# A hybrid decoder step on one core: the output projection taken by weight chunk, V caches loaded by chunk, and six smaller moves of loads and work

## The reference

```python
z = rmsnorm(x, g_mix) @ w_in                 # 1024 -> 3592 columns
attn_out = attn_fn(heads(aq), ak, av)        # 8 heads, mixture of windows (128,1) (512,4) (2048,16)
h_m, C, n, m = mlstm_chunked(...)            # 4 heads, matrix memory
h_h, S_new = hgrn2_chunked(...)              # 4 heads, gated linear recurrence
mlstm_out = sigmoid(mo) * head_rmsnorm(h_m, mlstm_g)
hgrn_out = sigmoid(hg) * head_rmsnorm(h_h, hgrn_g)
x = x + concat([attn_out, mlstm_out, hgrn_out]) @ w_out      # 1024 x 1024
u = rmsnorm(x, g_ffn) @ w_up                                 # 1024 -> 4096
x = x + square(relu(u)) @ w_down                             # 4096 -> 1024
```

## Time and profile before

| | |
|---|---|
| time, median of 3 runs | 1718.2 us (1717.47 to 1721.23) |
| the profiled execution's own time | 1717.58 us |
| its span | 1715.7 us |
| mean granted clock of TensorE | 0.967 of full |
| busy: PE, DVE, ACT, POOL | 91%, 50%, 28%, 14% of the span |

### The profile page before, as it was taken

How to read it: one execution, slowest core, us unless ns; L and a number is a source line. 1 busy time by engine, 2 the same in 40 slices (tenths; PEclk the granted TensorE clock), 3 DMA queues, 4 the chain that set the end, 5 groups by cost and what they waited for, 6 DMA issues and landing times.

```text
span 1715.7 us, 25329 instructions
## 1 busy us (share of the span) xinstructions
PE 1566.2 (91%) x10513; PEld 1372.4 (80%) x10513; DVE 857.8 (50%) x1493; ACT 480.1 (28%) x942; POOL 238.8 (14%) x341
## 2 busy tenths in 40 slices
PE   4899999799999798877499899999999999999997
PEld 3899889698889566663378788888889888888886
DVE  4682544066664277642734444444444444444446
ACT  4342221222211267631421322122122222212213
POOL 4421111687621000000500000000000000000000
PEclk9899999899999899989699999999999999999999
DMA  5322002712111832068300211111111111111102
GB/s 159 126 71 53 26 13 49 85 55 68 36 45 52 307 125 70 21 229 344 98 30 1 89 50 50 50 50 50 35 39 49 38 50 37 50 50 50 50 1 102
DMA packets 101268, 126.52 MB, mean 74 GB/s; under 512 B 27042, under 2 KB 78818, under 8 KB 99106
## 3 DMA queue, kind: packets, MB, share of 16 engines
q1 hardware_dynamic: 99090, 120.17, 22.5%
q0 software_dynamic: 2064, 4.72, 0.7%
HBM read 110.61 MB, written 18.98 MB: 76 GB/s over the span
## 4 chain that ended last, share of the span: by engine, by line
PE 51%; DVE 3%; DMA 1%; SPq 1%; ACT 0%; issue 0%; POOL 0%; DVEq 0%; POOLq 0%; ACTq 0%
PE PS L331 16%; PE PS L333 16%; PE PS L332 16%; PE PS L341 1%; PE PS L1739 1%; DVE R_wo L1913 1%; SPq L1722 1%; DMA R_cache<-in_cache_attn_v 1%; DVE R_x L2219 1%; DMA R_epb<-in_c_other_batch 1%; PE PS L1749 1%; DVE R_x L2245 0%; PE PS L1775 0%; PE PS L2039 0%; SPq L1723 0%
## 5 line engine op out<-in xcount | busy, mean ns | idle before, releaser
L331 PE MATMUL PS<-x_high,R_up 128*128 128x352 f32 x768 | 250.0, 326 | 4.8 <-DVEq L288 4.8
L333 PE MATMUL PS<-x_high,R_up 128*128 128x352 f32 x768 | 248.2, 323 | 0.0
L332 PE MATMUL PS<-x_low,R_up 128*128 128x352 f32 x768 | 247.4, 322 | 0.0
L2245 DVE TENSOR_TENSOR R_x<-R_x,PS 128x512 f32<-128x512 f32 (+1 forms) x272 | 182.0, 671 | 123.3 <-PE PS L333 117.5
L2191 ACT ACTIVATE R_usq<-R_upos 128x352 f32<-128x352 f32 x96 | 47.9, 499 | 562.9 <-issue 364.8
L331 PE MATMUL PS<-R_down,R_u 128*128 128x512 f32 x512 | 202.0, 395 | 0.0
L333 PE MATMUL PS<-R_down,R_u 128*128 128x512 f32 x512 | 201.6, 394 | 0.0
L332 PE MATMUL PS<-R_down,R_u 128*128 128x512 f32 x512 | 201.1, 393 | 0.0
L2234 DVE TENSOR_SCALAR R_upos<-PS 128x352 f32<-128x352 f32 x96 | 50.4, 525 | 260.9 <-PE PS L333 260.9
L331 PE MATMUL PS<-xn_high,R_w 128*128 128x352 f32 x408 | 138.3, 339 | 18.0 <-ACT R_spill L745 9.1
L331 PEld LDWEIGHTS PS<-x_high,R_up 128*128 128x128 f32 x768 | 144.6, 188 | 11.2 <-issue 6.2
(11 more groups left out here) (348 smaller groups left out, 2713.8 us busy)
## 6 DMA issues: line engine op xcount, KB each, us to landing
R_raw<-in_w_down SPq DMA_DIRECT2D x32, 512.0 KB, 4.5
R_stage<-in_w_up SPq DMA_DIRECT2D x30, 512.0 KB, 3.7
R_wstage<-in_w_in SPq DMA_DIRECT2D x28, 512.0 KB, 3.9
R_cache<-in_cache_attn_k SPq DMA_DIRECT2D x8, 1024.0 KB, 9.9
R_cache<-in_cache_attn_v SPq DMA_DIRECT2D x8, 1024.0 KB, 9.7
R_cache<-in_cache_attn_k SPq DMA_DIRECT2D x24, 256.0 KB, 7.8
R_cache<-in_cache_attn_v SPq DMA_DIRECT2D x24, 256.0 KB, 7.2
bias_by_distance_copies<-bias_by_distance POOLq DMA_DIRECT2D x1, 4608.0 KB, 27.9
```

Source lines behind the costliest of these rows:

```text
L331: pe.matmul(out, ll, rh, start=(k == 0), stop=False)
L332: pe.matmul(out, lh, rl_, start=False, stop=False)
L333: mm = pe.matmul(out, lh, rh, start=False, stop=(k == n - 1))
L2245: dve.tensor_tensor(part, part, PS[:, 4 + j % 4, 0:w], ALU.add).then_inc(d_taken, 1)
```

## The change

- HGRN state loads: at t = 21 only the mLSTM states are stored; the level masks follow at t = 22, two HGRN state loads at t = 23 and two at t = 24.
- A third `AS` buffer, in free columns of `R_spill`; DVE's mask step j waits for the use of j-3 and no longer of j-2.
- Side bias for head pair 0 too, loaded at the end of phase b into `R_pb4`; G itself is loaded first in phase c. The K caches of sequences 0 to 2 come next, then the tables of the key bias, then cache 4; cache 3 comes after the key bias is made, since `R_keys` now lies in its slot.
- The key bias is made in steps 3 and 4 of phase c.
- The table `bother` lies in `small` and is loaded in phase c.
- V caches are loaded block by block: 56 DMAs of 256 KB, each as soon as the K block in its place has been transposed.
- Output projection: tiles 0 and 1 are accumulated together, chunk k of w_out by chunk k, in four PSUM pairs; tile 2 is whole in f1. In f2 the transposes stand elsewhere, two pieces of the first up product (`hidden_piece`) are made between them, and the barrier behind f2 is gone. In block 0 of the MLP the pieces are ordered token group by token group.

The core of the diff (line numbers of rows below are those of the kernel before):

```diff
@@ d_sync
+            if t == 22:
                 sp.wait_ge(st_out, 16 * 8)
                 sp.dma_start(lev, const("c_levels")).then_inc(h_in, 16)
                 sp.dma_start(bmask2, const("c_batch")).then_inc(h_in, 16)
+            if t in (23, 24):
                 for a, h2, pt in halves():
-                    sp.dma_start(Sss[pt, :, a, :], i_["state_hgrn_S"][0, :, 2 * a + h2].rearrange("b k v -> k b v"))\
-                      .then_inc(h_in, 16)
+                    if a == t - 23:
+                        sp.dma_start(Sss[pt, :, a, :], i_["state_hgrn_S"][0, :, 2 * a + h2].rearrange("b k v -> k b v"))\
+                          .then_inc(h_in, 16)
@@ decayed_scores
-                if j >= 2:
-                    dve.wait_ge(am_used, j - 1)
+                if j >= 3:
+                    dve.wait_ge(am_used, j - 2)
...
-                dve.tensor_reduce(AS[j % 2][0:r, 0:r], AM[0:r, l0:, 0:r].rearrange("p l t -> p t l"), AX.X, ALU.add)\
+                dve.tensor_reduce(AS[j % 3][0:r, 0:r], AM[0:r, l0:, 0:r].rearrange("p l t -> p t l"), AX.X, ALU.add)\
@@ phase_c_sync
+            bias_in(0)
+            bias_side_in(sp, 1)
+            load_caches(sp, (0, 1, 2))
             sp.dma_start(keyrows, const("c_bias_keys")).then_inc(e_in, 16)
             sp.dma_start(keymask, const("c_key_mask")).then_inc(e_in, 16)
+            sp.dma_start(bother, const("c_other_batch")).then_inc(e_in, 16)
             for t in range(NT):
                 sp.dma_start(ra[32 * t:32 * t + 32, :], i_["rel_bias"]).then_inc(e_in, 16)
-            sp.wait_ge(bias_copies, 16)
-            bias_in(0)
-            bias_side_in(1)
-            load_caches(sp, range(NAHEAD))
+            load_caches(sp, (4,))
@@ phase_c_pe
+                if p == KEY_BIAS_AT + 1:
+                    pe.wait_ge(bkey_ready, 2)
...
+                if p == KEY_BIAS_AT:
+                    pe.wait_ge(e_in, 112)
+                    pe.wait_ge(rexp_ready, 1)
+                    for n in range(2):
+                        mm = pe.matmul(PS[:, 4 + n, 0:NKEY // 2], rexp, keyrows[:, n * (NKEY // 2):(n + 1) * (NKEY // 2)],
+                                       start=True, stop=True)
+                    mm.then_inc(bkey_psum, 1)
@@ phase_e
-            sp.dma_start(bother, const("c_other_batch")).then_inc(e_in, 16)
-            load_caches(sp, range(NSLOT, 2 * NSLOT))
+            stream_values(sp)
...
+        def stream_values(sp):
+            for g in range(2):
+                for k in range(NKT):
+                    for b in range(4 * g, 4 * g + 4):
...
+                        sp.wait_ge(kt_psum, 4 * (g * NKT + k) + b % 4 + 1)
+                        sp.dma_start(cache[b][:, k, :], src).then_inc(cache_in[b], 16)
@@ phase_f1_pe
+            f1_transposed(pe, 0)
+            f1_transposed(pe, 1)
+            for k in range(KD):
+                if k % 4 == 0:
+                    pe.wait_ge(f_split, mix_order(1, k // 4))
+                if k in (5, 6):
+                    f1_transposed(pe, k - 3)
+                pe.wait_ge(chunk_split, NW + k + 1)
+                for i in range(2):
+                    for n in range(2):
+                        projection_step(pe, i, n, k)
+            f1_transposed(pe, 4)
+            f1_transposed(pe, 5)
+            output_projection(pe, 2)
@@ output_projection
+            for n in range(2):
+                for k in range(KD):
+                    projection_step(pe, i, n, k)
+                if i == 2 and n == 0:
+                    for j in range(6, NTILE):
+                        f1_transposed(pe, j)
@@ phase_f2_pe
+            project(3)
+            normalised_transposed(0)
+            project(4)
+            normalised_transposed(1)
+            project(5)
+            normalised_transposed(2)
+            normalised_transposed(3)
+            for i in (6, 7, 8):
+                project(i)
+                normalised_transposed(i - 2)
+            hidden_piece(pe, 0, 0)
+            pe.wait_ge(x1_in, 16 * 13)
+            pe.wait_ge(sumsq_ready, 2 * NTILE)
+            pe.matmul(PS[:, 7, 0:1], token_sum, stat[:, 0, NCH:NTILE], start=True, stop=True).then_inc(token_psum, 1)
+            normalised_transposed(NCH - 1)
+            hidden_piece(pe, 0, 1)
+            normalised_transposed(NCH)
@@ phase_g_sync
+            sp.wait_ge(op_psum, 2 * NCH + 1)
+            sp.wait_ge(norm_split, 2 * NTILE)
             sp.dma_start(grow, i_["g_final"].rearrange("(o d) -> o d", o=1).to_broadcast([P, D])).then_inc(x1_in, 16)
@@ hidden_piece
+            if U < NU:
+                pe.wait_ge(norm_split, (6, 12, 2 * NTILE)[g])
+            if 2 <= U < NU:
+                pe.wait_ge(f_taken, 3 * NTILE + 13 + U)
+            if U >= 4:
+                pe.wait_ge(u_relu, U - 3)
@@ run
-                if n != 4:
+                if n not in (4, 5):
                     barrier(eng, name)
```

More of the change, by code:

```diff
@@ L1925, in attended, with after_f1, mix_order, mix_high @@
             return mixa[:, :, tile_tokens(j)] if j < NCH else atts
+        def after_f1(n):
+            return 2 * NTILE + n
+        def mix_order(j, kk):
+            return after_f1((2 * kk + j if j < 2 else 2 * j + kk) + 1)
         def phase_f1_act(act):
+            def mix_high(j, kk):
+                ks, ts = half(j, kk)
+                if kk:
+                    act.wait_ge(f_taken, after_f1(j + 1))
+                act.activation(XH[:, ks, ts], tmp4[j % 2] if kk else attended(j), ACT.Copy).then_inc(f_high, 1)
             for n, (pt, cs) in enumerate(PARTS):
@@ L1952, in phase_f1_dve, with mix_low @@
-        def phase_f1_dve(dve):
+            for m in range(KD):
+                chunk_high_part(act, m)
+                if m < 2:
+                    mix_high(m, 0)
+                if m in (3, 5):
+                    mix_high(m // 2 - 1, 1)
+            for j in range(2, NCH):
+                for kk in range(2):
+                    mix_high(j, kk)
+        def phase_f1_gps(pool):
+            def mix_low(j, kk):
+                ks, ts = half(j, kk)
+                pool.wait_ge(f_high, mix_order(j, kk))
+                pool.tensor_tensor(XL[:, ks, ts], tmp4[j % 2] if kk else attended(j), XHf[:, ks, ts], ALU.subtract)\
+                    .then_inc(f_split, 1)
+            for kk in range(2):
+                for j in range(2):
+                    mix_low(j, kk)
+            for j in range(2, NCH):
+                for kk in range(2):
+                    mix_low(j, kk)
@@ new lines, in phase_f1_dve, with scaled, with_gain @@
+        def phase_f1_dve(dve):
+            def scaled(i):
+                r = rows(i)
+                for w in range(2):
+                    part = (mo, hg)[w][0:r, i, :].rearrange("p (h e) -> p h e", e=E)
+                    ins = dve.tensor_tensor(part, part, hrstd[0:r, w, i, :].unsqueeze(2).to_broadcast([r, HM, E]), ALU.mult)
+                ins.then_inc(f_scaled, 1)
+            def with_gain(j):
+                dve.wait_ge(f_psum, j + 1)
+                if 2 <= j < NCH:
+                    dve.wait_ge(f_split, mix_order(j - 2, 1))
+                dst = tmp4[j % 2] if j < NCH else xr[:, 4:8]
+                dve.tensor_tensor(dst, PS[:, j % 2, :].rearrange("p (k t) -> p k t", t=P)[:, :, 0:rows(j)],
+                                  gout[:, 4:8].unsqueeze(2).to_broadcast([P, 4, rows(j)]), ALU.mult).then_inc(f_taken, 1)
@@ L1978, in phase_f1_pe @@
[L1978 to L1991 removed]
+            scaled(0)
@@ new lines, in phase_f1_dve @@
+            scaled(1)
+            chunk_low_part(dve, 0)
+            chunk_low_part(dve, 1)
+            with_gain(0)
+            chunk_low_part(dve, 2)
+            with_gain(1)
+            chunk_low_part(dve, 3)
+            scaled(2)
+            chunk_low_part(dve, 4)
+            scaled(3)
+            chunk_low_part(dve, 5)
+            chunk_low_part(dve, 6)
+            with_gain(2)
+            chunk_low_part(dve, 7)
+            with_gain(3)
+            for i in (4, 6):
+                scaled(i)
+                scaled(i + 1)
+                with_gain(i)
+                with_gain(i + 1)
@@ new lines, in phase_f1_dve, with f1_transposed @@
+            scaled(NCH)
+            dve.tensor_copy(xr[:, 0:4], atts)
+            with_gain(NCH)
+        def f1_transposed(pe, i):
+            r = rows(i)
+            pe.wait_ge(f_scaled, i + 1)
+            if i >= 2:
+                pe.wait_ge(f_taken, after_f1(i - 1))
+            for k in range(4):
+                t = pe.transpose(PS[:, i % 2, k * P:k * P + r], (mo, hg)[k // 2][0:r, i, k % 2 * P:(k % 2 + 1) * P],
+                                 ident[0:r, 0:r])
+            t.then_inc(f_psum, 1)
@@ new lines, in op_bank, with projection_step @@
+        def op_bank(i, n):
+            return {0: 4, 1: 6, 2: 2}.get(i, 4 + 2 * ((i + 1) % 2)) + n
+        def projection_step(pe, i, n, k):
+            ts, ns = tile_tokens(i), slice(n * 512, (n + 1) * 512)
+            out = PS[:, op_bank(i, n), :]
```

(5 more changed lines are left out.)

242 lines of the change are left out of this document (104 added, 138 removed).

## The result

The changed kernel takes 1669.47 us (median; 1662.69 to 1674.72) where the kernel before took 1719.72 us on the same chip: ratio 0.9719, 95% interval 0.9684 to 0.9753, faster. 1664.5 was predicted, with a range of 1655 to 1674. Two later measurements of the unchanged code gave 0.9718 (0.9694 to 0.9741) and 0.9717 (0.9701 to 0.9733).

What follows compares the result with a forecast made beforehand. PE, busy 91% of the span, bounds the kernel, so only idle time and low clock can be gained. Terms 5.5 + 0.3 + 8.6 + 16.5 + 22.5 = 53.4 off 1717.6, plus 0.3 for the median: 1664.5 us, range 1655 to 1674.

Steps and rivals of the forecast that it cites:

- State loads: Phase b, spreading state DMAs around the level masks: level scores start earlier, 5.5 us gained, bounds 3.5 to 7.6.
- The mask then becomes the last to matter: Phase b: mask load issued at about 307.5 lands by 321.3, against 324.9 before, so at least 3.5 us gained.
- Third buffer: Wait on `R_as`: DVE's mask step is late behind its state update, so another buffer gains only 0.3 us, bounds 0 and 3.
- The rival at 1653: Wait on `R_as`: the added score buffer removes all 11.6 us of wait, giving 1653; chance 0.06.
- Start of c: First steps of phase c: earlier biases and G bring step 3's scores 11.1 us forward, less key bias cost: 8.6 us gained.
- Mask and V stream: Phase e: early mask table saves 9.0 us, block-wise V loads bring the second product forward: 16.5 us gained, bounds 9 and 17.
- the rival's condition (385): Phase e: V streaming under about 385 GB/s makes the second product wait; gain falls to 9 to 10, 1672; chance 0.12.
- Projection and tail: Start of f1 to first down product: earlier projection start and fewer holes on PE, 22.5 us gained, bounds 17 and 26.
- the gaps: f1 to first down product: PE waits of 3, 1, 2 and 2.5 us at four places, together 8.5.
- The moves in b and c: Phases b and c: another DMA, of mask or G, is late next; together 9 us less, 1673; chance 0.04.
- The signs: Expected trace evidence: L745 wait under 10 us, level scores near 333, `R_as` waits remaining, no V wait, f1 nearly without holes.
- The slower rival: f1 and f2, 822 to 962 us: TensorE at half clock, up to 131 us more, 1795; chance 0.02.

Runs made afterwards that it cites:

- the run above: Changed kernel with the key bias tables issued ahead of the K caches in phase c and phase b's state stores spread over slots: 1662.38 us, ratio 0.9698.

## Why the prediction was right, and where its terms were not

The forecast held: faster, inside the range, and in e and behind it by the mechanisms named. In b and c the thing moved came early and another DMA was late in its place. The gain is 50.3 us of medians against 53.4 forecast (47.7 in the profiled span). That it came so near is in part luck: three terms were too high, by 3.4, 3.2 and 1.8 us, and the last was too low by 3.4.

- **State loads: 5.5 forecast, 2.1 measured (2.7 and 3.5 in the other two executions).** The step that failed is the lower bound: "The mask then becomes the last to matter", landed at 321.3 at the latest. The last to matter is the store that was moved ahead of it, which landed 15.3 us after its issue, behind the eight state stores. With these spread, 5.5 us more came, 7.6 in all, and POOL's work bounded the rest. The Trainium skill, "DMA: Bandwidth & Descriptors", section "Specifications", gives 512 bytes as the least transfer for line rate. The trace agrees in part: with 6364 of 8030 packets under it the rate was 99 GB/s, but stores with rows of 256 bytes alone landed in 2.5 us, and only those with 4-byte rows between them took 10.9.
- **Third buffer: 0.3 forecast.** Shown by the run with two buffers. The rival at 1653 is out.
- **Start of c: 8.6 forecast, 5.4 measured.** The early part was right (scores of step 3 11.6 us early against 11.1). Mis-sized was "0.4 if its tables, queued behind three caches, come late": that lateness cost 3.7. With the tables first the term is 9.1, and the work of the moved key bias 2.5, as taken (2.6).
- **Mask and V stream: 16.5 forecast, 14.7 measured** (16.5 in the third execution). The mask is worth 11.3 by itself, more than the 9.0 counted, since the K part also kept its clock. The stream adds 3.4 to that (87.7, 76.4, 73.0), or 4.8 when it is undone in the changed kernel, not 7.5. "At the 412 GB/s of the window" was too high: from 742 to 775 us the blocks moved mostly at 383 to 397 GB/s, where whole caches had 407 in the run with the mask alone. DMA of the changed kernel, 723 to 782 us, in 40 slices:

```profile
DMA  0698899999999999999999999999999999999989
GB/s 11 193 293 308 315 264 364 418 392 432 421 397 397 389 383 387 386 387 386 389 387 386 386 393 343 353 392 394 387 385 392 386 386 387 386 387 371 257 335 408
```

  This is 5% less with rows of 2 KB, and at the edge of the rival's condition (385). The packets in the traces agree: one of 2 KB took 88 ns on its engine here, one of 8 KB 310 ns in the run with the mask alone, so four small ones take 352 for the same bytes. At 387 GB/s the 14.7 MB take 38.0 us, 2.4 more than the 35.6 counted, about the 2.67 us that PE stood. So the rival's wait came, but not its price: "the term falls to 9 to 10" would have left 77 to 78 us in phase e. The Trainium skill, "Perfetto Trace Analysis", section "DMA Optimizations", prefers larger transfers for throughput. The trace agrees in sign: they had 407 GB/s against 387; the early start still won.
- **Projection and tail: 22.5 forecast, 25.9 measured.** It is made of two parts. The first projection starts 4.0 us behind the first head transposes in place of 22.0: 18.0 us, as forecast (4.1). From there to the first down product it takes 137.1 us in place of 144.9: 7.8 us, where the forecast had 4.6. Mis-sized are the gaps: 8.5 forecast; in the trace 2.67 before the last head transposes, 0.50 before the down product, none before the hidden piece or piece 4. With the 131.4 us of work that the prediction counts and 3.2 of waits, 2.5 are left, most of it the first 5 us at half clock. (The prediction's own sum is 962.1, not 962.5.) Undone one by one, the barrier gives back 3.5, the order by chunk 4.0, DVE's order 1.3; in all three runs the first projection still starts 4.0 us behind the head transposes. So none of the three made the 18.0 us. What all three keep is the rest of the order: before, PE had the transposes of tiles 2 and 3 ahead of the first projection, they waited for a gain that stood behind all eight low parts (17.23 us), and the projection itself waited for all low parts and for the second half of x, which POOL made only after nine first halves. Now the projection waits for one low part and the first halves of two tiles, and those transposes stand between chunks. That this is the cause is read from the wait that is gone; no run put it back.
- **The moves in b and c.** The rival "another DMA, of the mask or of G, is late next" had 0.04 and a price of 9 us. Its mechanism came in both phases, though with other DMAs: the store of slot 48 in b and the tables of the key bias in c. Both terms together gave 7.5 us in place of 14.1, 6.6 less. That the time still fell near the forecast is due to the last term; this rival was given too little.
- **The signs.** ACT's wait at L745 was to be under 10 us and the level scores near 333; they were 13.55 and 339.42 (3.1 us of this is the later start of the stage). The second group with V was not to wait and to take 6.2 us; it waited 2.67 and took 7.71. The prediction names that wait as a sign that it is too low; it was, by 5.0 us. The signs on `R_as`, on the first steps of c, on the mask and on f1 held.
- **The slower rival.** It did not come. In f1 the clock was at half from 796 to 805 us and at full from about 805 on, in spite of the waits; from 820 to 850 us its mean was 0.94 and from 850 to the first down product 1.00.

## What to carry to other kernels

A wait that names a buffer says what was late, not why: follow the engine that writes it back to what it did before. When a DMA is moved ahead of another, count what is queued ahead of it still, and look at the row size of each of those transfers, not at their bytes: here 8 KB in rows of 4 bytes are the likely cause of a 15 us delay. When an edit is undone to see what it was worth, look whether the wait that it was meant for comes back; in f1 it did not. When a wait goes, look for what the clock gives back as well: it was 2.3 us on 9.0 here.

## What the runs showed of the hardware

**The clock falls in a busy stretch too.** Windows of the changed kernel in phase b:

```profile
200.00:204.00 4.00, 3.94 (x30) 1.00 0.00 0
204.00:208.00 4.00, 4.00 (x23) 0.57 0.00 0
208.00:212.00 4.00, 3.94 (x32) 1.00 0.00 0
```

PE has 3.94 us or more of work in each 4 us, and the granted clock goes to 0.57, that is to 1.2 of 2.4 GHz for most of these 4 us, and comes back. Between 180 and 300 us this happens six times in this execution, five and four times in the second and third of the same code, and three times in the kernel before. With it the copy ahead of the stall moved by 4.6 us between executions of the same code, and one stage by 5 us in the run above. What sets it off is open; no run varied it. It makes a single profile's total uncertain by some 5 us, so the edits here are sized by stages.

**DVE and POOL slow each other.** A low part of 128x1024 took 2.3 us beside POOL's subtractions in the earlier trace rows and 1.2 us without them in the run with low parts whole, the same operation on the same tiles. The Trainium skill, "SBUF — State Buffer", section "Who interferes with whom", says that the two share a port pair that one of them holds alone at a time. The numbers nearly agree: side by side one of each started every 2.2 us (the six in the middle of the earlier trace rows); by themselves the low parts started every 1.14 us and POOL's subtractions 1.25 us apart (at 814.88 and 816.13 us of that run), 2.39 together. So all but some 0.2 us of a pair ran one after the other.
